# A chunked recurrence in twelve slots per pair of heads: the side work moved behind the state product, and row steps exchanged between VectorE and GpSimd

## The chip, the cores and the metric

The kernel runs on one core of a Trainium2 chip. The metric is the device time of one execution in microseconds (us), as the median of a few runs. The profile is one further execution, recorded by the hardware profiler. Engine names in its rows: PE is TensorE (matmuls), PEld its weight loads, DVE is VectorE, ACT is ScalarE, POOL is GpSimd, SP only issues DMAs.

## The reference, cut to what matters

The program is two transformer blocks. The change touches one stage of the second: the bidirectional recurrence (RWKV-7) over 768 tokens (512 of the sequence, 256 of a context) for 16 heads of width 64. Token by token, and for both directions, the reference computes:

```python
kk = heads(k * k_k);  kk = kk / maximum(norm(kk), 1e-12)
kt = heads(k)[None] * (1 + (a - 1) * heads(k_a))
sk = einsum('bhij,bhj->bhi', S, kk)                       # one step
S  = S * w - sk[..., None] * kka + v[..., None] * kt
y  = einsum('bhij,bhj->bhi', S, r)
```

where `kka` is `kk * a`. The outputs `y` of both directions are added, normalised per head, scaled and shifted (`ln_g`, `ln_b`), a bonus `(r * kt * r_k) summed * v` is added, and all is multiplied by a gate `g`.

## The kernel before

The 16 heads are worked two at a time: eight *pairs*, p = 0 to 7 (`RW_PAIRS`). Within a pair the 768 tokens are cut into twelve chunks of 64, in both directions at once. A chunk is one *slot*, i = 0 to 11 (`RW_STEPS`). A slot carries the state of the recurrence on, and that is a chain that no order can shorten:

1. PE multiplies the state with the chunk's keys (`scan_u`, matmuls L3651);
2. DVE adds the chunk's own part and gives `u` (`scan_u`, L2773);
3. PE forms the state product from `u` (`scan_states`, L3678) and, in slots 4 to 11, the outputs (L3662, L3666, L3685);
4. DVE adds it to the state (L2780) and multiplies by the decay (L2783), and the next slot can begin.

Beside this chain each engine works for the next pair, n = p + 1, and in part for the one after, m = p + 2. Everything is written out by hand: each engine's program is a fixed list, and semaphores tie the lists together. There is no scheduler. `beside_values(p, i)` is what stands between `scan_u` and the state product of slot i, and `beside_states(p, i)` what stands behind the state product. The PSUM banks are handed out by a plan in the same order (`plan_recurrence`).

The side work for a pair, in the order in which it depends on itself:

- DVE makes unit keys (`unit_keys`, four parts, L2675 to L2684) in slots 5 to 8 of the pair before the previous one.
- GpSimd (`factors`, L1421 to L1426) forms `kk * a` and `k * (1 + (a - 1) * k_a)` for both directions, 768 elements a partition, then three products for the bonus (`weigh_bonus`, L1433 to L1435).
- PE makes cumulated decays by matmul (`side` with "sum" and "sum_ex", L3527 and L3531), ACT takes their exponentials (L1804 to L1808), DVE scales keys, factors and r by them (`scale`, L2703), PE turns the results (`side`, L3539) and ACT copies them out (L1812).
- In slot 3 PE forms the 32-row blocks (`blocks_of`, L3560), DVE masks them (L2724, L2732) and transposes them (L2737).
- GpSimd inverts the blocks by row steps (`invert_blocks`, L1446 and L1447: 30 steps of a multiply and a subtract, 30 to 240 elements a partition, each waiting for the one before).
- In slot 10 DVE transposes the result twice (`turn_blocks`, L2744 and L2745), and `join`, `inverse` and `solved` on PE and ACT (L3573, L3584, L3596, L3602) make of it what the slots of the next pair read.
- DVE reads out the pair before (`read_out` in five parts, L2797 to L2818) and forms v times bonus (`weigh_values`, L2767, L2768).

Where an instruction waits on a result of its own engine the helper `link` puts a semaphore between the two. The buffer `products_kept` holds both the bonus products and the temporary of the row steps; the keys `kk` and the untransposed `blocks` share their memory.

Of the kernel before, what the change touches and what calls it, by code (L numbers as in the profile page):

```python
# [18 lines left out]
ALU = mybir.AluOpType  # L19
# [399 lines left out]
RW_SCALED = [("K", 0), ("R", 0), ("B", 0), ("T", 0), ("B", 1), ("K", 1), ("R", 1), ("T", 1)]  # L419
# [10 lines left out]
def plan_recurrence(plan, norm):  # L430
# [26 lines left out]
    def beside_values(p, i):  # L457
# [3 lines left out]
        if i == 0:  # L461
            if goes_on:
                side(n, "R", 0, 2)
            if p >= 0:
                plan.add("act", "rw_x", p, 1, width=4, bank=4)
        elif i == 1:
            if p >= 0:
                plan.add("act", "rw_inv", p, 1, width=4, bank=4)
            if goes_on:
                side(n, "T", 0, 2)  # L470
        elif i == 2:
            if p >= 0:
                solved(p, 1)
            if goes_on:
                side(n, "B", 1, 2)
        elif i == 3 and goes_on:
            plan.add("dve", "rw_lead", n, width=2, bank=4)
            plan.add("act", "rw_off", n, width=2, bank=6)
        elif i == 4 and p >= 0:
            plan.add("act", "rw_inv", p, 2, width=4, bank=4)  # L480
        elif i == 5 and p >= 0:
            solved(p, 2)
        elif i == 6 and goes_on:
            plan.add("act", "rw_gv", n, 0, width=2, bank=6)
# [8 lines left out]
    def beside_states(p, i):  # L493

        n = p + 1
        goes_on = n < RW_PAIRS
        if i == 0 and goes_on:
            side(n, "B", 0, 2)
            side(n, "sum", 1, 6)
        elif i == 1 and goes_on:  # L500
            side(n, "sum_ex", 1, 2)
        elif i == 2:
            if goes_on:
                side(n, "K", 1, 2)
            if p >= 0:
                plan.add("act", "rw_x", p, 2, width=4, bank=4)
        elif i == 3 and goes_on:
            plan.add("dve", "rw_tail", n, width=2, bank=4)
            side(n, "R", 1, 2)
        elif i == 4 and goes_on:  # L510
            side(n, "T", 1, 4)
        elif i == 5 and goes_on:
            plan.add("dve", "rw_g", n, 0, width=2, bank=4)
        elif i == 6 and goes_on:
            plan.add("dve", "rw_g", n, 1, width=2, bank=6)
        elif i == 7 and goes_on:
# [14 lines left out]
    for p in range(-1, RW_PAIRS):  # L531
        for i in range(RW_STEPS):
            if p >= 0:
                plan.add("dve", "rw_u", p, i, bank=0)
            beside_values(p, i)
            if p >= 0:
                scan_states(p, i)
            beside_states(p, i)
# [92 lines left out]
def build(nc, a, out, debug=None):  # L631
# [438 lines left out]
    def _(sp):  # L1070
# [14 lines left out]
        def load_beside(p):  # L1085
# [6 lines left out]
            if m < RW_PAIRS:  # L1092
# [4 lines left out]
                sp.wait_ge(sem("rw_factors"), factored(n, "T", 1))  # L1097
# [6 lines left out]
                sp.wait_ge(sem("rw_scaled"), rw_scaled(n, "T", 1))  # L1104
# [92 lines left out]
    def _(pool):  # L1197
# [211 lines left out]

        def factors(p, z):  # L1410
# [11 lines left out]
            pool.wait_ge(sem("rw_factors"), factored(p, "B", z))  # L1422
# [3 lines left out]
            G.tensor_tensor(az, az, RW_IN["k"], ALU.mult).then_inc(sem("rw_factors"), 1)  # L1426

        def weigh_bonus(p):
# [3 lines left out]
            pool.wait_ge(sem("rw_factors"), factored(p, "T", 1))  # L1432
# [4 lines left out]
        def invert_blocks(p):  # L1437

            pool.wait_ge(sem("rw_blocks_turned"), p + 1)
            link(G.memset(Y.rearrange("p c r -> p (c r)")[:, 0:SUB * SUB:SUB + 1], -1.0))  # L1440
            pool.wait_ge(sem("rw_bonus_ready"), p + 1)
            for j in range(1, SUB - 1):
                shape = [P, j, SUB - 1 - j]
                rest = Y[:, 0:j, j + 1:SUB]
                kept = products_kept.rearrange("p t d -> p (t d)")[:, 0:j * (SUB - 1 - j)].rearrange("p (c r) -> p c r", c=j)
                link(G.tensor_tensor(kept, Y[:, j:j + 1, j + 1:SUB].to_broadcast(shape), Y[:, 0:j, j:j + 1].to_broadcast(shape), ALU.mult))  # L1446
                ins = G.tensor_tensor(rest, rest, kept, ALU.subtract)  # L1447
                if j < SUB - 2:
# [2412 lines left out]
```

## Time and profile before

| | us |
|---|---|
| runs (three) | 4464.9, 4474.24, 4474.59 |
| median | 4474.24 |
| profiled execution | 4468.43 |
| its span on the core | 4467.1 |
| busy in the span: PE / DVE / ACT / POOL | 3969.7 / 1493.4 / 1030.2 / 1244.3 |
| the recurrence: from the first state (pair 0) to the first state of pair 7 | 639.2, seven pairs |

Outside the recurrence PE is busy for nine tenths of nearly every slice of the span. Inside it PE falls to six or seven tenths, and the granted clock of PE with it. The rest of the 4467 us is not touched by the change. A pair's start can be found in the trace by the memset of the state (L2788), a slot's start by the add that gives `u` (L2773).

### The profile page before, as it was taken

Reading aid. Unit: us, or ns where it says so; the run is one execution under the profiler, and the core shown is the slowest. Engines: PE = TensorE matmul, PEld = TensorE weight load, DVE = VectorE, ACT = ScalarE, POOL = GpSimd, SP = SyncE. Lnnn points to the kernel's source line nnn. Section 1 sums busy time; section 2 is a strip of 40 time slices with the busy share of each in tenths; the row PEclk is TensorE's granted clock in tenths of the full one; section 3 lists DMA queues with packets and bytes.
Section 4 is the critical chain, followed back from the end, with each engine's and each line's share of the span. In section 5 each row is a group of like instructions: output and inputs, shape, how many; then the busy total and the mean of one; then the engine's idle time right before and its main releaser. Section 6 shows DMA issues by size and latency. Waiting matters only on the chain.

```text
span 4467.1 us, 80505 instructions
## 1 busy us (share of the span) xinstructions
PE 3969.7 (89%) x34715; PEld 2496.1 (56%) x34715; DVE 1493.4 (33%) x2904; ACT 1030.2 (23%) x2164; POOL 1244.3 (28%) x1239
## 2 busy tenths in 40 slices
PE   8999999998999899997999998997566677769999
PEld 7977887877887444663333333444445555433443
DVE  4333332333243220553100115024455555342223
ACT  1032111002201221551212222113333333131111
POOL 4324323423344102110011110115666566010000
PEclk9999999999999999998999999998777777789999
DMA  4244212222222212552899996325011110169999
GB/s 152 88 169 148 83 60 75 76 99 82 84 94 81 65 57 59 161 156 102 309 344 344 348 346 252 101 96 173 28 31 38 46 35 10 46 250 409 408 406 368
DMA packets 277214, 701.52 MB, mean 157 GB/s; under 512 B 27488, under 2 KB 78080, under 8 KB 276608
## 3 DMA queue, kind: packets, MB, share of 16 engines
q1 hardware_dynamic: 250608, 637.58, 38.9%
q0 software_dynamic: 26256, 58.79, 4.9%
q8 instruction: 279, 4.57, 0.4%
q14 instruction: 71, 0.58, 0.0%
HBM read 654.61 MB, written 38.93 MB: 155 GB/s over the span
## 4 chain that ended last, share of the span: by engine, by line
PE 34%; POOL 6%; issue 5%; DVE 4%; DMA 4%; ACT 2%; SPq 0%; POOLq 0%; DVEq 0%; ACTq 0%
PE banks L3384 9%; PE banks L2951 6%; PE banks L3410 4%; DMA ring<-in_moe_w 3%; PE banks L3394 3%; POOL arena L1447 2%; POOL arena L1446 2%; PE banks L3357 2%; PE banks L3704 1%; PE banks L3418 1%; PE banks L3502 1%; ACT arena L1727 1%; PE banks L3493 1%; PE banks L3527 1%; PE banks L3475 1%
## 5 line engine op out<-in xcount | busy, mean ns | idle before, releaser
L2951 PE MATMUL banks<-ring,arena 128*128 128x512 f32 x1248 | 541.8, 594 | 0.4 <-DVE arena L2435 0.4
L2992 PE MATMUL banks<-arena 128*128 128x256 f32 x2256 | 507.7, 381 | 6.0 <-DVE arena L1990 6.0
L3384 PE MATMUL banks<-ring,arena 128*64 128x512 f32 x2048 | 471.4, 600 | 13.0 <-DMA ring<-in_moe_w 6.9
L2992 PEld LDWEIGHTS banks<-arena 128*128 128x128 f32 x2256 | 436.6, 200 | 61.3 <-issue 5.5
L2951 PEld LDWEIGHTS banks<-ring,arena 128*128 128x128 f32 x1248 | 236.0, 191 | 288.6 <-issue 285.8
L2992 PE MATMUL banks<-ring,arena 128*128 128x256 f32 x1584 | 356.3, 383 | 1.6 <-DVE arena L2299 1.6
L2992 PEld LDWEIGHTS banks<-ring,arena 128*128 128x128 f32 x1584 | 314.9, 216 | 35.6 <-DVE arena L2299 2.4
L3384 PEld LDWEIGHTS banks<-ring,arena 128*64 128x64 f32 x2048 | 140.2, 137 | 325.8 <-issue 318.0
L1249 POOL TENSOR_TENSOR arena<-ring 128x1024 f32<-128x1024 f32 x47 | 117.1, 2491 | 642.9 <-PE banks L2992 627.2
L2992 PE MATMUL banks<-arena,ring 128*128 128x256 f32 x1280 | 283.0, 379 | 1.2 <-ACT arena L1579 0.7
L3410 PE MATMUL banks<-ring,arena 128*64 128x512 f32 x1024 | 262.6, 665 | 6.9 <-ACT arena L1748 6.6
L2992 PEld LDWEIGHTS banks<-arena,ring 128*128 128x128 f32 x1280 | 243.2, 190 | 35.6 <-issue 1.4
L2589 DVE TENSOR_TENSOR arena<-banks,arena 64x512 f32<-64x512 f32 x64 | 44.4, 694 | 566.0 <-ACT arena L1741 566.0
L1741 ACT ACTIVATE arena<-banks 64x512 f32<-64x512 f32 x64 | 37.7, 589 | 591.6 <-PE banks L3384 591.6
L3410 PEld LDWEIGHTS banks<-ring,arena 128*64 128x64 f32 x1024 | 81.9, 152 | 153.3 <-issue 143.1
L2562 DVE TENSOR_TENSOR arena<-arena,banks 128x512 f32<-128x512 f32 x112 | 70.7, 683 | 257.3 <-PE banks L3357 257.3
L1447 POOL TENSOR_TENSOR arena<-arena 128x30 f32<-128x30 f32 (+14 forms) x240 | 144.5, 602 | 18.8
L1258 POOL TENSOR_TENSOR arena<-ring,arena 128x1024 f32<-128x1024 f32 x47 | 119.5, 2543 | 98.2 <-PE banks L2992 96.3
L1990 DVE TENSOR_TENSOR arena<-arena 128x1024 f32<-128x1024 f32 x55 | 116.8, 2124 | 85.8 <-PE banks L2992 80.7
L1446 POOL TENSOR_TENSOR arena<-arena 128x30 f32<-128x30 f32 (+14 forms) x240 | 133.8, 558 | 18.8
L3539 PE MATMUL banks<-ident,arena 64*64 64x64 f32 x2816 | 80.1, 279 | 66.3 <-DVE arena L2703 53.4
L1727 ACT ACTIVATE arena<-banks,mod,mod_a 128x64 f32<-128x64 f32 (+1 forms) x384 | 117.5, 422 | 65.8 <-PE banks L3311 35.5
(460 smaller groups left out, 5750.5 us busy)
## 6 DMA issues: line engine op xcount, KB each, us to landing
ring<-in_moe_w SPq DMA_DIRECT2D x768, 512.0 KB, 8.9
ring<-in_w_in SPq DMA_DIRECT2D x21, 2048.0 KB, 7.7
ring<-in_ada_w SPq DMA_DIRECT2D x12, 2048.0 KB, 8.0
ring<-in_ada_w SPq DMA_DIRECT2D x24, 1024.0 KB, 5.6
ring<-in_w_up SPq DMA_DIRECT2D x8, 2048.0 KB, 8.6
ring<-in_w_down SPq DMA_DIRECT2D x8, 2048.0 KB, 7.8
ring<-in_na_w_qkv SPq DMA_DIRECT2D x6, 2048.0 KB, 8.0
ring<-in_w_in SPq DMA_DIRECT2D x8, 1024.0 KB, 6.4
```

The costliest lines, as they stand in the source:

```text
L1249: nc.gpsimd.tensor_tensor(s1, a21, a22, ALU.add).then_inc(sem("weights_added"), 1)
L1258: nc.gpsimd.tensor_tensor(s4, a12, s2, ALU.subtract).then_inc(sem("weights_added"), 1)
L1446: link(G.tensor_tensor(kept, Y[:, j:j + 1, j + 1:SUB].to_broadcast(shape), Y[:, 0:j, j:j + 1].to_broadcast(shape), ALU.mult))
L1447: ins = G.tensor_tensor(rest, rest, kept, ALU.subtract)
L1727: ins = A(x_chosen[:, b, 4 * half + k, lo:hi], ps[:, k, lo:hi], ACT.Identity, bias=shift, scale=scale)
L1990: V.tensor_tensor(to, x, y, ALU.subtract).then_inc(sem("tokens_added"), 1)
L2951: ins = mm(ps[:, 0:ncol], lhs(k), rhs(k), start=(k == 0 and first), stop=(k == nk - 1))
L2992: ins = mm(ps[:, HW * j:HW * (j + 1)], lhs[:, k, j, :] if len(lhs.shape) == 4 else lhs[:, k, P * j:P * (j + 1)], rhs[:, k, :], start=(star ...
L3357: ins = mm(open_("moe_add", l, e, kind, t, n), selT[rows, b, t * P:(t + 1) * P], y_l[rows, b, :], start=True, stop=True)
L3384: ins = mm(ps, x_chosen[:, b, k, 0:CAP_L], w[x][:, n * W:(n + 1) * W], start=(k == 0), stop=(k == KD - 1))
L3394: ins = mm(ps[r:r + CAP_C, :], x_chosen[:, b, k, CAP_L:SLOTS], w[:, n * W:(n + 1) * W], start=(k == 0), stop=(k == KD - 1))
L3410: ins = mm(ps, hidT[:, k, 0:CAP_L], w[:, n * W:(n + 1) * W], start=(k == 0), stop=(k == KD - 1))
```

## The change

Three things change.

First the order. `beside_values` and `beside_states` become one `beside(p, i)` on every engine, behind the state product:

```diff
             for i in range(RW_STEPS):
                 if p >= 0:
                     scan_u(p, i)
-                beside_values(p, i)
-                if p >= 0:
                     scan_values(p, i)
                     scan_states(p, i)
-                beside_states(p, i)
+                beside(p, i)
```

Some products move to another slot with it: "sum_ex" of direction 1 from slot 1 to 0, "B" of direction 0 from 0 to 1, "T" of direction 0 from 1 to 2, the tail blocks stand right behind the lead blocks in slot 3, `join(p, 2)` goes from slot 2 to 1, "sum" and "sum_ex" of pair m to slots 8 and 9, its "K" to slot 10.

Second the row steps go from GpSimd to DVE, cut over slots 4 to 9:

```diff
-        def invert_blocks(p):                                  # GpSimd
...
+        def invert_blocks(p, lo, hi):                          # VectorE
+            if lo == 1:
+                dve.wait_ge(sem("rw_blocks_turned"), p + 1)
+            for j in range(lo, hi):
...
+                link(V.tensor_tensor(kept, Y[:, j:j + 1, j + 1:SUB].to_broadcast(shape), Y[:, 0:j, j:j + 1].to_broadcast(shape), ALU.mult))
+                link(V.tensor_tensor(rest, rest, kept, ALU.subtract))
```

Third, streaming work goes from DVE to GpSimd: the weighing of the keys, their scaling to unit length, the scaling of "T" of direction 1, the last three products of the read-out and the two of v times bonus. In `factors` two operations with a constant become operations with a tensor:

```diff
-            link(G.tensor_scalar(az, az, -1.0, None, ALU.add))
             link(G.tensor_tensor(az, az, across(k_a, NT), ALU.mult))
-            link(G.tensor_scalar(az, az, 1.0, None, ALU.add))
-            G.tensor_tensor(az, az, RW_IN["k"], ALU.mult)
+            link(G.tensor_tensor(az, az, across(k_a, NT), ALU.subtract))
+            link(G.tensor_tensor(az, az, RW_IN["k"], ALU.mult))
+            G.tensor_tensor(az, az, RW_IN["k"], ALU.add)
...
-        for p in range(RW_PAIRS):
-            factors(p, 1)
-            weigh_bonus(p)
-            invert_blocks(p)
-            if p + 1 < RW_PAIRS:
-                factors(p + 1, 0)
+        for p in range(-1, RW_PAIRS):
+            n, m = p + 1, p + 2
+            if n < RW_PAIRS:
+                factors(n, 1)
+                scale_values(n)
+                weigh_bonus(n)
+            if m < RW_PAIRS:
+                weigh_keys(m)
+                scale_keys(m)
+            if p >= 1:
+                read_out(p - 1)
+            if p >= 0:
+                weigh_values(p)
+            if m < RW_PAIRS:
+                factors(m, 0)
```

`weigh_keys(m)` waits for `rw_blocks_turned` of pair n (slot 3), `scale_keys(m)` for the new semaphore `rw_key_scales` (DVE, slot 8), `read_out` for `rw_y_scaled` (DVE, slot 8), `factors(m, 0)` for PE's "sum_ex" of pair m (slot 9), `factors(n, 1)` for the last output of pair n - 2. The waits of ACT, PE and SP on the scaled "T" of direction 1 now name the semaphore of the factors.

On PE, slot 3 of one pair before, with the end of slot 2; L3651 is the product that opens a slot, L3560 the blocks, L3678 the state product, L3539 a turned operand:

```order
L3678 MATMUL banks<-ring,arena 64x64 x4
L3678 MATMUL banks<-arena 64x64 x4
L3539 MATMUL banks<-ident,arena 64x64 x24
L3573 MATMUL banks<-arena 32x32 x16
L3651 MATMUL banks<-arena,ring 64x128 x2
L3560 MATMUL banks<-arena 32x32 x96
L3678 MATMUL banks<-ring,arena 64x64 x4
L3678 MATMUL banks<-arena 64x64 x4
L3560 MATMUL banks<-arena 32x32 x48
L3539 MATMUL banks<-ident,arena 64x64 x16
L3651 MATMUL banks<-arena,ring 64x128 x2
```

The same place in the changed kernel (L3661 opens the slot, L3570 the blocks, L3688 the state product, L3549 a turned operand):

```order
L3606 MATMUL banks<-arena,ring 64x64 x16
L3612 MATMUL banks<-ring,arena 64x64 x16
L3549 MATMUL banks<-ident,arena 64x64 x48
L3661 MATMUL banks<-arena,ring 64x128 x2
L3688 MATMUL banks<-ring,arena 64x64 x4
L3688 MATMUL banks<-arena 64x64 x4
L3570 MATMUL banks<-arena 32x32 x144
L3661 MATMUL banks<-arena,ring 64x128 x2
```

The 96 block products that stood between `u` and the state product now stand behind it, together with the other 48.

On DVE, slot 8 of a pair before; L2773 to L2783 are the chain, L2682 to L2684 the keys, L2811 to L2813 the read-out:

```order
L2773 TENSOR_TENSOR arena<-banks,ring 128x128
L2780 TENSOR_TENSOR arena<-banks,arena 128x256
L2783 TENSOR_TENSOR arena<-arena 128x256
L2682 TENSOR_SCALAR rw_s<-rw_s 128x12
L2683 RECIPROCAL rw_s<-rw_s 128x12
L2684 TENSOR_TENSOR arena<-arena,rw_s 128x768
L2811 RECIPROCAL rw_s<-rw_s 128x8
L2812 TENSOR_TENSOR ring<-ring,rw_s 128x512
L2813 TENSOR_TENSOR ring<-ring,arena 128x512
```

Slot 8 in the changed kernel, up to its third row step (L2797 to L2807 are the chain, L2767 and L2768 the row steps, of which this slot has seven):

```order
L2797 TENSOR_TENSOR arena<-banks,ring 128x128
L2804 TENSOR_TENSOR arena<-banks,arena 128x256
L2807 TENSOR_TENSOR arena<-arena 128x256
L2705 TENSOR_SCALAR rw_s<-rw_s 128x12
L2706 RECIPROCAL rw_s<-rw_s 128x12
L2835 RECIPROCAL rw_s<-rw_s 128x8
L2836 TENSOR_TENSOR ring<-ring,rw_s 128x512
L2767 TENSOR_TENSOR arena<-arena 128x234
L2768 TENSOR_TENSOR arena<-arena 128x18x13
L2767 TENSOR_TENSOR arena<-arena 128x228
L2768 TENSOR_TENSOR arena<-arena 128x19x12
```

Two wide operations have left the slot and fourteen small ones have come.

On GpSimd, what stands in the changed kernel from the bonus products on (L1410 and L1416 the keys, L1464 to L1466 the read-out, L1455 and L1456 v times bonus, L1427 to L1432 the factors); before, the 60 row steps followed the bonus products here, and then the factors:

```order
L1448 TENSOR_TENSOR arena<-arena 128x512
L1410 TENSOR_TENSOR arena<-ring,arena 128x768
L1416 TENSOR_TENSOR arena<-arena,rw_s 128x768
L1464 TENSOR_TENSOR ring<-ring,arena 128x512
L1465 TENSOR_TENSOR ring<-ring,arena 128x512
L1466 TENSOR_TENSOR ring<-ring 128x512
L1455 TENSOR_TENSOR arena<-ring,arena 128x512
L1456 TENSOR_TENSOR arena<-arena 128x512
L1427 TENSOR_TENSOR ring<-arena,ring 128x768
L1429 TENSOR_TENSOR ring<-ring,arena 128x768
L1430 TENSOR_TENSOR ring<-ring,arena 128x768
```

Everything GpSimd does for a pair is now wide operations with two tensors as inputs, 21 of them.

## Rows read from the trace of the kernel before

**Rows 1.** Windows: PE, PEld, DVE, ACT, POOL busy us (count), clock, DMA share, GB/s.

```profile
3167.88:3807.06 639.18, 433.74 (x12360) 343.92 (x12360) 356.79 (x537) 212.84 (x445) 409.38 (x516) 0.73 0.12 35
3361.82:3384.91 23.09, 15.29 (x464) 11.54 (x464) 13.34 (x19) 8.98 (x18) 7.25 (x5) 0.84 0.27 84
3384.91:3396.84 11.93, 7.93 (x372) 6.75 (x372) 4.74 (x8) 1.72 (x5) 0.00 (x0) 0.50 0.05 18
3396.84:3421.19 24.35, 18.51 (x588) 15.35 (x578) 16.84 (x28) 9.24 (x20) 21.50 (x37) 0.83 0.06 19
3421.19:3427.30 6.11, 4.12 (x72) 3.56 (x72) 5.22 (x11) 1.73 (x4) 5.56 (x8) 0.72 0.01 3
3427.30:3431.41 4.11, 3.72 (x33) 1.95 (x33) 3.13 (x5) 2.46 (x5) 3.72 (x6) 0.69 0.00 0
3431.41:3441.86 10.45, 5.38 (x60) 3.86 (x60) 6.40 (x8) 2.69 (x6) 9.34 (x16) 0.83 0.12 39
3441.86:3450.96 9.10, 6.17 (x205) 5.19 (x208) 3.72 (x5) 4.27 (x10) 8.84 (x5) 0.78 0.17 46
```

**Rows 2.** Waits from 3167.88 to 3807.06: us in total, times, longest.

```profile
POOL arena L1440 <- DVE arena L2737: 185.0, 7, 29.4
DVE arena L2780 <- PE banks L3678: 134.4, 70, 4.2
DVE arena L2773 <- PE banks L3651: 75.3, 30, 6.5
```

**Rows 3.** Timeline, DVE, opening of slot 8: start, duration, what, idle before.

```profile
3421.19 0.28 DVE L2773 TENSOR_TENSOR arena<-banks,ring 128x128 f32<-128x128 f32 x1
3422.12 0.43 DVE L2780 TENSOR_TENSOR arena<-banks,arena 128x256 f32<-128x256 f32 x1 [0.65 <-PE banks L3678]
3422.58 0.75 DVE L2783 TENSOR_TENSOR arena<-arena 128x256 f32<-128x256 f32 x1
```

**Rows 4.** One line's instructions on DVE: duration ns min/median/max, first and last start.

```profile
L2711 DVE TENSOR_TENSOR arena<-arena x16: 172/488/1799, 3100.3 to 3746.3; 128x24 f32<-128x24 f32 x16
L2780 DVE TENSOR_TENSOR arena<-banks,arena x88: 414/425/426, 3179.0 to 3872.1; 128x256 f32<-128x256 f32 x88
L2703 DVE TENSOR_TENSOR arena<-arena x24: 958/961/2487, 3086.8 to 3745.4; 128x768 f32<-128x768 f32 x24
```

**Rows 5.** Groups on POOL, same stretch: count, busy us, mean ns, idle before.

```profile
L1424 POOL TENSOR_TENSOR ring<-ring,arena 128x768 f32<-128x768 f32 x14 | 25.4, 1817 | 1.2
L1446 POOL TENSOR_TENSOR arena<-arena 128x240 f32<-128x240 f32 x14 | 8.8, 631 | 1.1
```

**Rows 6.** Timeline, DVE and POOL in slot 0.

```profile
3362.53 1.81 POOL L1426 TENSOR_TENSOR ring<-ring 128x768 f32<-128x768 f32 x1
3363.61 1.00 DVE L2783 TENSOR_TENSOR arena<-arena 128x256 f32<-128x256 f32 x1
3364.48 1.26 POOL L1433 TENSOR_TENSOR arena<-ring 128x512 f32<-128x512 f32 x1
3364.65 3.67 DVE L2703 TENSOR_TENSOR arena<-ring,arena 128x768 f32<-128x768 f32 x2
3365.82 1.69 POOL L1434 TENSOR_TENSOR arena<-arena,ring 128x512 f32<-128x512 f32 x1
3367.59 1.87 POOL L1435 TENSOR_TENSOR arena<-arena 128x512 f32<-128x512 f32 x1
```

**Rows 7.** Timeline, DVE and POOL in slot 0 of the next pair.

```profile
3453.96 2.18 POOL L1425 TENSOR_SCALAR ring<-ring 128x768 f32<-128x768 f32 x1
3454.19 2.33 DVE L2703 TENSOR_TENSOR arena<-ring,arena 128x768 f32<-128x768 f32 x2
3456.22 1.96 POOL L1426 TENSOR_TENSOR ring<-ring 128x768 f32<-128x768 f32 x1
3456.44 1.79 DVE L2711 TENSOR_TENSOR arena<-arena 128x24 f32<-128x24 f32 x1
```

**Rows 8.** Timeline, DVE ahead of pair 0.

```profile
3163.84 1.97 DVE L2744 STREAM_TRANSPOSE arena<-arena 128x1024 f32<-128x1024 f32 x1 [20.23 <-POOL arena L1447]
```

More of the change, by code:

```diff
@@ L465, in beside_values @@
                 plan.add("act", "rw_x", p, 1, width=4, bank=4)
+            if goes_on:
+                side(n, "sum", 1, 4)
+                side(n, "sum_ex", 1, 6)
         elif i == 1:
+            if goes_on:
+                side(n, "B", 0, 2)
             if p >= 0:
                 plan.add("act", "rw_inv", p, 1, width=4, bank=4)
+                plan.add("act", "rw_x", p, 2, width=4, bank=4)
             if goes_on:
-                side(n, "T", 0, 2)
+                side(n, "B", 1, 2)
         elif i == 2:
@@ new lines, in beside @@
+            plan.add("dve", "rw_g", n, 2, width=2, bank=4)
+        elif i == 8:
+            if goes_on:
+                plan.add("act", "rw_gv", n, 2, width=2, bank=6)
+            if n + 1 < RW_PAIRS:
+                side(n + 1, "sum", 0, 4)
+        elif i == 9 and n + 1 < RW_PAIRS:
+            side(n + 1, "sum_ex", 0, 6)
+        elif i == 10:
+            if n + 1 < RW_PAIRS:
+                side(n + 1, "K", 0, 6)
+            if p >= 1 and goes_on:
+                plan.add("act", "rw_ot", p - 1, bank=4)
@@ L1408, in across, with weigh_keys, scale_keys @@
             return row.unsqueeze(1).to_broadcast([P, nt, P])
+        def weigh_keys(p):
+            loaded(pool, "k", p)
+            loaded(pool, "rows", p)
+            if p >= 1:
+                pool.wait_ge(sem("rw_blocks_turned"), p)
+                pool.wait_ge(sem("rw_scaled"), rw_scaled(p - 1, "K", 1))
+            G.tensor_tensor(kk, RW_IN["k"], across(rw_rows[:, 0, :], NT), ALU.mult).then_inc(sem("rw_keys_weighed"), 1)
+        def scale_keys(p):
+            pool.wait_ge(sem("rw_key_scales"), p + 1)
+            keys = kk.rearrange("p t (h d) -> p (t h) d", d=HD)
+            G.tensor_tensor(keys, keys, rw_s[:, 0:12].unsqueeze(2).to_broadcast([P, 12, HD]), ALU.mult).then_inc(sem("rw_keys_ready"), 1)
+            pool.wait_ge(sem("rw_keys_ready"), p + 1)
         def factors(p, z):
@@ L1460, in _ @@
+        read_out(RW_PAIRS - 1)
         taken(pool, "rw_ot", RW_PAIRS - 1)
@@ L1877, in beside_values @@
                     joined(p, 1)
+                if goes_on:
+                    side(n, "sum", 1)
+                    side(n, "sum_ex", 1)
             elif i == 1:
+                if goes_on:
+                    side(n, "B", 0)
                 if p >= 0:
                     inverse(p, 1)
+                    joined(p, 2)
                 if goes_on:
-                    side(n, "T", 0)
+                    side(n, "B", 1)
             elif i == 2:
@@ L2900, in _ @@
                     scan_u(p, i)
-                beside_values(p, i)
-                if p >= 0:
                     scan_state(p, i)
-                beside_states(p, i)
-        for part in range(1, 6):
+                beside(p, i)
+        for part in range(1, 5):
             read_out(RW_PAIRS - 1, part)
@@ L3716, in beside_values @@
                     join(p, 1)
+                if goes_on:
+                    side(n, "sum", 1)
+                    side(n, "sum_ex", 1)
             elif i == 1:
+                if goes_on:
+                    side(n, "B", 0)
                 if p >= 0:
                     inverse(p, 1)
+                    join(p, 2)
                 if goes_on:
-                    side(n, "T", 0)
+                    side(n, "B", 1)
             elif i == 2:
@@ L3725, in beside_values @@
                 if goes_on:
-                    side(n, "B", 1)
+                    side(n, "K", 1)
+                    side(n, "T", 0)
             elif i == 3 and goes_on:
@@ L3741, in beside_values @@
                 group_values(n, 1)
-            elif i == 10 and n + 1 < RW_PAIRS:
-                side(n + 1, "sum_ex", 0)
+                rb_products(n, 2)
+                g_products(n, 2)
+            elif i == 8:
+                if goes_on:
+                    group_values(n, 2)
+                if n + 1 < RW_PAIRS:
+                    side(n + 1, "sum", 0)
+            elif i == 9 and n + 1 < RW_PAIRS:
+                side(n + 1, "sum_ex", 0)
+            elif i == 10:
+                if n + 1 < RW_PAIRS:
+                    side(n + 1, "K", 0)
+                if p >= 1 and goes_on:
+                    read_out(p - 1)
             elif i == 11 and goes_on:
```

365 lines of the change are left out of this document (149 added, 216 removed).

## The prediction

> **What bounds the kernel now.** I read the page first: PE is nine tenths busy nearly everywhere but in the recurrence, so only there can a new order be worth anything. Then the windows. From the first state of pair 0 to that of pair 7 seven pairs take 639.2 us, 91.3 us each; in them PE is busy 434, POOL 409, DVE 357 [rows 1]. No engine is full, so the pair is bound by a chain that changes engine. The seven further windows cut one pair at its slots (3361.82 to 3450.96, 89.1 us): slots 0 to 3 take 35.0 us (23.1 and 11.9), slots 4 to 9 34.6 us (24.35, 6.11 and 4.11), slots 10 and 11 19.55 us [rows 1].
>
> The waits say which chain. DVE waits for the state product 134.4 us in 70 slots, 1.92 us a slot, and for the product that gives `u` another 75.3 us [rows 2]. Where nothing stands between `u` and the state product the first wait is 0.65 us [rows 3]. So 1.27 us a slot is PE's side work in front of the state product: 12.7 us for the ten such waits of a pair. POOL is no bound: it waits 26.4 us a pair for the blocks [rows 2], and takes 58.5 [rows 1]. But a faster pair would run into it: 60 row steps of up to 0.63 us [rows 5] must fit between slot 3 and slot 10.
>
> **The change part by part.**
>
> *The order.* It takes away at most the 12.7 us above. Not all comes back: the products still have to be made, now beside DVE's side work. In slots 0 to 3, 10 and 11 PE and ACT set the end; by the windows they take 54.55 us. In slot 3 PE is busy 7.9 of 11.9 us, and behind its last block DVE still has to mask and transpose; slot 0 now also gets "sum_ex". I credit half of 12.7, 6.3 us, there. What it gives in slots 4 to 9 is in the next sum, which starts from nothing but DVE's work.
>
> *Row steps on DVE.* Prices: 24 elements take 0.17 us, 256 take 0.425, 768 take 0.96 [rows 4]; that is 0.15 us and 1.05 ns an element, and 0.04 us to the next linked operation (L2780 ends at 3422.55, L2783 stands at 3422.58 [rows 3]). Thirty steps of j x (31 - j) elements, twice, are 9920 elements: 10.4 us, and 60 x 0.19 = 11.4 us, together 21.8 us of DVE a pair. Off DVE go two operations of 768 for the keys, one of 768 for "T", three of 512 for the read-out, two of 512 for v times bonus: 3 x 0.96 + 5 x 0.69 = 6.3 us at undisturbed prices. DVE's total of 51 us a pair [rows 1] becomes some 66.
>
> Slots 4 to 9 hold all of it. A slot there costs DVE the chain, 0.28 + 0.65 + 0.43 + 0.04 + 0.42 = 1.82 us [rows 3], and then its side work, since `u` of the next slot stands behind that. Six chains are 11; row steps 21.8; masks, key sums and the three read-out parts that stay, 10.7 (three masks of 512, two double ones, two operations of 768, six of 512 or small). That is 43.5 us where the windows show 34.6: 8.9 us worse. With the 6.3 us above, a pair without any disturbance between DVE and POOL is 2.6 us longer.
>
> *Streaming on POOL.* This decides. In slot 0 DVE and POOL take turns. L2783, 0.42 us alone, takes 1.00, until POOL's L1426 ends at 3364.34; two L2703 of 0.96 take 3.67, while POOL's 1.09 and 1.26 us operations become 1.69 and 1.87 [rows 6]. Twenty-four elements take 1.79 us and end with POOL's operation [rows 7]. So an operation with two SBUF inputs on one engine waits out such an operation on the other, and between two of one the other gets its turn. Each POOL operation that falls among row steps therefore delays DVE by its own length, 1.82 [rows 5] or 1.26 us [rows 6], plus 0.08 to the next, less the 0.45 us of the DVE operation that fits in: 1.45 us at 768 wide, 0.9 at 512.
>
> Where do they fall? `weigh_keys` waits for the transposed blocks: slot 4, one operation, 1.45. `scale_keys`, three of the read-out and two of v times bonus are released by DVE in slot 8, in front of its 14 row operations: 1.45 + 5 x 0.9 = 5.95, and slot 8 has enough operations to meet all six. `factors(m, 0)` starts when PE has done "sum_ex" in slot 9, when three or four of the 12 row operations there are left, and goes on under the transposes of slot 10: 4.0 (between 1 and 7). Slots 0 to 2 see such operations before and after. Sum 11.4 us a pair. All of it is on the path: PE's side work in slots 8 and 9 is 4 us or less, and `u` is queued on DVE behind the row steps.
>
> The low end of this term is 0, if the operations miss each other or POOL does not get a turn inside a linked row; the high end is all that POOL does between slot 8 and slot 10, 1.82 + 5 x 1.26 + 1.54 + 4 x 1.82, 17 us. I take 11.4, which is rows 6 applied as it stands.
>
> The Trainium skill (SBUF — State Buffer, SBUF: two separate sides) has DVE and GpSimd share a port pair as an exclusive lock for a whole instruction, against any GpSimd operation that reads SBUF. By that the constants' operations held DVE just as well, and replacing them changes nothing. The trace disagrees in part: beside the one-input L1425 two L2703 took 2.33 us, not 1.92 and a wait of 2 us [rows 7]. By the page some of my slot 9 term was paid before too, and the sum would be up to 2 us a pair lower, 4541; by the row four operations a pair are new blockers, and 4555 stands.
>
> *Head and tail.* Ahead of pair 0 DVE waits 20.2 us for POOL's row steps [rows 8]. They shrink from about 38 (3126 to 3163.8) to 21.8 plus what stands between them on DVE, some 10; but the unit keys of pair 0 now wait for POOL, about 4 us. I take -4, between -18 and +5. The last read-out waits for three POOL operations of 1.26 instead of 0.69: +2.
>
> *Sum.* Pairs 1 to 5: 2.6 + 11.4 = 14, times five, 70. In pair 0 there is no read-out, 14 - 2.7 = 11.3. In pair 6 there is no pair m: no keys, five POOL operations at 0.9 against 3.5 us less on DVE, about +4. Together 85, with head and tail 83. On the profiled execution (4468.4) that is 4551; the median of the runs lies 6 us above it, so I say 4555 against 4474.
>
> **The rivals.**
>
> *A, faster: the chain was the bound and DVE has room.* Mechanism: in every slot PE's side work now runs beside DVE's, and POOL's wide operations fall on DVE's PSUM reads and waits, not among the row steps. Price: -12.7 in full against +8.9, -3.8 a pair, 27 us in seven, and 15 us of the 20.2 us at the head: 4432. For it: 134 us of waits at the state product. Against: the row steps are two-input operations nearly back to back. It decides if slot 8 takes 9 us or less.
>
> *B, the exchange is even: no turns taken, but DVE is full in slots 4 to 9.* 7 x 2.6 - 2: +16, 4490. For it: POOL's 34 us a pair leave it idle most of the time.
>
> *C, worse: POOL gets late.* `read_out` and `factors(m, 0)` are delayed by DVE as DVE is by them; if `factors(n, 1)` then begins only in slot 0, the scaling of "B" and PE's turned operands wait too. Price: the whole 17 us instead of 11.4, and some 4 us in slots 0 to 2: 10 more a pair, 4620.
>
> *D, nothing:* A and B cancel within 0.3% (13 us, what a measurement of this kernel can tell), around 4474.
>
> **How the numbers follow.** Forecast 0.53, its own range 4510 to 4595. A 0.21, B 0.11, C 0.07, D 0.08. Faster by over 0.3%: A, 0.21. Within: D, 0.08. Slower: the rest, 0.71. The range to hold eight in ten goes from 4440, inside A, to 4600.
>
> **What the changed profile would show.** Right: the wait of DVE for the state product near 0.65 us in nearly every slot; slot 8 of a middle pair 13 to 17 us with POOL and DVE durations alternating, row operations there over 1 us each where those of slots 6 and 7 are near 0.4; slots 5 to 7 between 7 and 8.5 us; slot 3 under 11; a pair of 103 to 107 us. POOL idle before `scale_keys`, not before anything else for long. Wrong: row operations in slot 8 near 0.4 us beside a busy POOL (then B), slots 0 to 3 under 28 us together (then A), or POOL releasing "B" late (then C). It would also be wrong if a linked row operation on DVE cost not 0.19 us and 1.05 ns an element: 0.1 us more each is 6 us a pair.

## The result and the profile after

| | before | after |
|---|---|---|
| median of four runs | 4469.57 us (4464.12 to 4474.59) | 4560.63 us (4552.72 to 4566.39) |
| profiled execution | 4468.43 us | 4566.39 us |
| span | 4467.1 us | 4565.0 us |
| first state of pair 0 | 3167.9 us | 3176.0 us |
| seven pairs | 639.2 us | 737.9 us |
| from the first state of pair 7 to the end | 660.0 us | 651.1 us |

The changed kernel is slower: ratio 1.0211, with a 95% interval of 1.019 to 1.0232. The forecast was 4555 us. The changed profiled execution is 98 us longer: 98.7 us more in the seven pairs, 8.2 more ahead of them, and 8.9 less behind them.

In what follows the line numbers of a kernel are its own: in the changed kernel `u` is L2797, the state's add L2804 and its decay L2807, the row steps are L2767 and L2768, `scale` is L2725, the state's memset L2812. A *turn* is what an operation of one vector engine loses while it waits for an operation of the other to end.

Page of the changed kernel, its first line: busy us, share of the span and instructions of each engine.

```profile
PE 3996.9 (88%) x34715; PEld 2533.2 (55%) x34715; DVE 1630.5 (36%) x3328; ACT 1031.4 (23%) x2164; POOL 1040.6 (23%) x815
```

Windows of the changed kernel, which answer to [rows 1]: the seven pairs, then pair 2 cut into slots 0 to 3, slots 4 to 9, slot 10 and slot 11.

```profile
3176.04:3913.92 737.88, 463.64 (x12372) 380.99 (x12372) 463.36 (x911) 213.15 (x445) 204.26 (x132) 0.67 0.10 31
3397.55:3431.72 34.17, 23.50 (x784) 18.67 (x784) 16.48 (x26) 9.51 (x18) 7.56 (x6) 0.70 0.23 74
3431.72:3481.69 49.97, 31.15 (x748) 25.44 (x748) 42.15 (x97) 15.70 (x33) 9.94 (x8) 0.76 0.04 10
3481.69:3494.79 13.10, 4.36 (x95) 3.73 (x92) 8.86 (x7) 2.41 (x6) 8.55 (x5) 0.56 0.01 1
3494.79:3503.34 8.55, 6.05 (x152) 4.85 (x148) 1.26 (x3) 3.45 (x9) 6.67 (x4) 0.50 0.16 48
```

DVE is busy 463 us in the seven pairs and was 357; POOL is down from 409 to 204. PE is busy 30 us more with the same products, at a granted clock of 0.67 against 0.73. The pair shown takes 105.8 us (pairs 1 to 5 take 105.7 to 109.1). Against the pair of [rows 1], slots 0 to 3 take 0.8 us less, slots 4 to 9 15.4 us more (DVE is busy for 42.15 of the 49.97 us), slots 10 and 11 2.1 us more. The pair of [rows 1] is the fastest of pairs 1 to 5 of its kernel. By the means of pairs 1 to 5 slots 4 to 9 again take 15.4 us more, and the other six slots 0.1 us less.

Waits in the changed kernel from 3176 to 3914, which answer to [rows 2]: us in total, times, longest.

```profile
POOL arena L1416 <- DVE rw_s L2706: 178.0, 6, 29.9
DVE arena L2797 <- PE banks L3661: 147.0, 41, 9.1
POOL arena L1410 <- DVE arena L2757: 136.5, 6, 24.7
DVE arena L2804 <- PE banks L3688: 61.7, 77, 2.2
POOL ring L1427 <- PE banks L3538: 59.6, 6, 11.2
POOL arena L1427 <- PE banks L3695: 34.2, 6, 5.9
```

The order did what it was to do: DVE waits 0.80 us a slot for the state product (61.7 us in 77 waits) where it waited 1.92. It waits for `u` instead, 147 us where it was 75. POOL is idle in front of both operations on the keys (L1410, L1416) and in front of the factors (L1427).

Timeline of the changed kernel, DVE and POOL in slot 8, which answers to [rows 3] and [rows 5], with one operation of slot 7 above it and `u` of slot 9 at its end.

```profile
3455.70 0.41 DVE L2767 TENSOR_TENSOR arena<-arena 128x238 f32<-128x238 f32 x1
...
3463.46 1.47 POOL L1416 TENSOR_TENSOR arena<-arena,rw_s 128x768 f32<-128x768 f32 x1 [29.72 <-DVE rw_s L2706]
3463.48 2.00 DVE L2836 TENSOR_TENSOR ring<-ring,rw_s 128x512 f32<-128x512 f32 x1
3465.61 1.31 POOL L1464 TENSOR_TENSOR ring<-ring,arena 128x512 f32<-128x512 f32 x1 [0.68 <-POOL arena L1416]
3465.82 1.35 DVE L2768 TENSOR_TENSOR arena<-arena 128x234 f32<-128x234 f32 x1
...
3468.38 1.30 POOL L1466 TENSOR_TENSOR ring<-ring 128x512 f32<-128x512 f32 x1
3468.59 1.34 DVE L2768 TENSOR_TENSOR arena<-arena 128x228 f32<-128x228 f32 x1
...
3470.91 1.29 POOL L1456 TENSOR_TENSOR arena<-arena 128x512 f32<-128x512 f32 x1
3471.11 1.33 DVE L2768 TENSOR_TENSOR arena<-arena 128x220 f32<-128x220 f32 x1
3472.48 0.38 DVE L2767 TENSOR_TENSOR arena<-arena 128x210 f32<-128x210 f32 x1
...
3475.61 0.29 DVE L2797 TENSOR_TENSOR arena<-banks,ring 128x128 f32<-128x128 f32 x1
```

Each row operation beside POOL lasts until POOL's operation is over, and ends 0.2 us after POOL's next one has started (3467.17 and 3467.00 the first time): 1.35 us for 234 elements, where 238 take 0.41 alone. Five are held for POOL's five operations of 512, and L2836 for `scale_keys`. When POOL is done, at 3472.2, the row operations are back at 0.38. The slot takes 14.56 us, from `u` at 3461.05 to `u` at 3475.61.

Slot 10, DVE and POOL, also of the changed kernel:

```profile
3481.39 1.54 POOL L1427 TENSOR_TENSOR ring<-arena,ring 128x768 f32<-128x768 f32 x1 [9.19 <-PE banks L3538]
3483.06 2.03 DVE L2807 TENSOR_TENSOR arena<-arena 128x256 f32<-128x256 f32 x1
...
3489.21 2.16 DVE L2725 TENSOR_TENSOR arena<-arena 128x768 f32<-128x768 f32 x1
3494.79 0.29 DVE L2797 TENSOR_TENSOR arena<-banks,ring 128x128 f32<-128x128 f32 x1 [3.42 <-PE banks L3661]
```

The factors begin at 3481.39, 0.2 us behind the last row operation of slot 9. So their turns fall on the decay, 2.03 us for 0.42, and on the scaling of "K", 2.16 for 0.96. Then DVE waits 3.42 us for `u`: PE has to transpose "K" in front of it, and "K" came only behind both of DVE's transposes.

PE transposing "K" in this slot (timeline of PE from 3481 to 3496), and a transposed operand at the end of slot 2 of the same pair (from 3415 to 3432):

```profile
3491.52 1.56 PE L3549 MATMUL banks<-ident,arena 64*64 64x64 f32 x48 [8.74 <-DVE arena L2725]
3417.76 0.92 PE L3549 MATMUL banks<-ident,arena 64*64 64x64 f32 x46 [0.25 <-issue]
```

PE had stood idle for 8.74 us when "K" came. From 3491.4 to the end of slot 11 the granted clock is 0.50, the lower of TensorE's two levels (1.2 GHz), and the 48 products take 1.56 us. Where the granted clock is 1.00 (3417.2 to 3418.6) 46 such products take 0.92. So part of the 3.42 us, and of slot 11's 8.55 us, is the slower clock behind the long wait.

### The profile page after: what moved, and what is told of

Same layout as the page of the kernel before. It is cut to its first block, busy times and chain, and to the rows that moved or that the text cites. A ratio compares the mean times of both kernels' runs of the same rounds, so it can differ in the third digit from the quotient of the medians.

```text
span 4565.0 us, 80518 instructions
## 1 busy us (share of the span) xinstructions
PE 3996.9 (88%) x34715; PEld 2533.2 (55%) x34715; DVE 1630.5 (36%) x3328; ACT 1031.4 (23%) x2164; POOL 1040.6 (23%) x815
## 4 chain that ended last, share of the span: by engine, by line
PE 35%; DVE 10%; DMA 5%; issue 3%; ACT 2%; POOL 1%; SPq 0%; DVEq 0%; POOLq 0%; ACTq 0%
PE banks L3391 9%; PE banks L2958 6%; DMA ring<-in_moe_w 4%; PE banks L3417 3%; PE banks L3401 3%; DVE arena L2768 2%; DVE arena L2767 2%; PE banks L3364 2%; PE banks L3549 1%; PE banks L3425 1%; PE banks L3534 1%; PE banks L3688 1%; PE banks L3714 1%; ACT arena L1755 1%; PE banks L3500 1%
## 5 line engine op out<-in xcount | busy, mean ns | idle before, releaser
L3549 PE MATMUL banks<-ident,arena 64*64 64x64 f32 x2816 | 80.4, 287 | 105.2 <-DVE arena L2725 89.0
L3688 PE MATMUL banks<-ring,arena 64*64 64x64 f32 x704 | 39.0, 290 | 131.7 <-DVE arena L2797 130.2
L3549 PEld LDWEIGHTS banks<-ident,arena 64*64 64x64 f32 x2816 | 73.5, 196 | 108.7 <-issue 93.4
```

The source lines that it names most:

```text
L3549: ins = mm(ps[to, c, t * CH:(t + 1) * CH], x[rows, t, to], ident[rows, rows], start=True, stop=True)
```

## The experiments

Ratios are against the kernel before, run beside on the same chip; its medians there were 4461.5 to 4465.8 us, so differences between medians of two experiments carry up to 8 us of that against 4469.57. Slot times are of one middle pair, where not called means. Since single executions reach the recurrence at times that differ by up to 8 us, its head is measured from GpSimd's memset of 128 x 256 just ahead of it (L1468 in the changed kernel): 80.1 us to the first state before, 88.4 us after. Means of pairs 1 to 5, in us:

| | slots 0 to 3 | 4 to 9 | 10 | 11 | all but 4 to 9 | pair |
|---|---|---|---|---|---|---|
| before | 35.8 | 35.3 | 10.8 | 10.0 | 56.7 | 91.9 |
| changed | 35.0 | 50.7 | 13.0 | 8.6 | 56.5 | 107.2 |
| `order_only` | 33.7 | 37.6 | 13.4 | 7.3 | 54.5 | 92.1 |
| `exchange_only` | 36.3 | 53.9 | 8.4 | 9.2 | 53.9 | 107.8 |
| `no_streak` | 34.7 | 46.6 | 12.9 | 8.6 | 56.2 | 102.8 |
| `no_rows` | 34.6 | 34.4 | 12.1 | 7.8 | 54.5 | 88.9 |
| `order_k_first` | 34.3 | 37.6 | 8.4 | 8.1 | 50.7 | 88.3 |
| `after_k_first` | 35.2 | 51.1 | 9.9 | 8.0 | 53.1 | 104.1 |
| `after_constants` | 35.3 | 50.7 | 10.8 | 7.7 | 53.8 | 104.5 |
| `read_out_back` | 35.2 | 49.7 | 12.2 | 7.7 | 55.1 | 104.8 |
| `three_together` | 34.8 | 49.6 | 7.9 | 7.1 | 49.8 | 99.4 |

**Order alone** (`order_only`). The order and tables of the change, with the row steps on GpSimd, the streaming work on VectorE and the constants in the factors as before:

```diff
 scan_u(p, i)
-beside_values(p, i)
 scan_state(p, i)
-beside_states(p, i)
+beside(p, i)
 # row steps, keys, read-out, v times bonus: as before
```

> The order of the changed kernel (side work behind the state product, the products in their new slots) with the old split of the work: row steps on GpSimd, keys, read-out and v times bonus on VectorE. The theory in the prediction (VectorE full in slots 4 to 9, and VectorE and GpSimd taking turns there, is what costs): the loss must be gone, 4445 to 4475 us, that is within 0.5% of before; not much below, because the 38 us of row steps on GpSimd then set the time from slot 3 to slot 10. Rival A (the order is worth its full 12.7 us a pair): 4385 or less. Rival (the new order itself is what loses, since 'K' of pair m now stands in slot 10 behind the transposes): 4500 or more.

Measured: 4452.88 us, ratio 0.9983 (0.9971 to 0.9996). The order is worth next to nothing as written. Slots 0 to 3 take 34.1 us, slots 4 to 9 37.2 (2.6 more than before), slot 10 13.7. By the means it gives 2.2 us a pair outside slots 4 to 9 and takes 2.4 inside them; what is left of it is 5.0 us at the head (75.1 for 80.1) and 8.8 from the first state of pair 7 on (651.3 for 660.0).

**Exchange alone** (`exchange_only`). The old order; row steps on VectorE, streaming work on GpSimd, factors without constants:

```diff
-invert_blocks(p)                 # GpSimd
+invert_blocks(p, lo, hi)         # VectorE, in slots 4 to 9
-read_out parts, weigh_values     # VectorE
+read_out, weigh_values           # GpSimd
```

> The exchange alone (row steps on VectorE, streaming on GpSimd, factors without constants) in the old order, with the row steps cut over slots 4 to 9 as in the changed kernel. Theory: it carries the whole loss and more, since PE's side work in front of the state product is not hidden either: 4560 to 4640. Rival (the order loses, the exchange is even): 4470 to 4500.

Measured: 4577.91 us, ratio 1.0271 (1.0252 to 1.0289). The whole loss is the exchange's; the order gives 0.6% of it back (1.0271 to 1.0211), most of it at the head (98.9 us here, 88.4 in the changed kernel) and little in a pair (107.8 and 107.2).

**Without GpSimd's streak** (`no_streak`). It leaves out the last three products of the read-out and the two of v times bonus, but for 8 columns of one tile:

```diff
-link(G.tensor_tensor(d, d, across(ln_rows[:, p % 2, 0, :], LT), ALU.mult))
-link(G.tensor_tensor(d, d, vb, ALU.add))
-G.tensor_tensor(d, d, RW_G[p % 2], ALU.mult)
+G.tensor_tensor(d[:, 0, 0:8], d[:, 0, 0:8], RW_G[p % 2][:, 0, 0:8], ALU.mult)
```

> The changed kernel with GpSimd's five 512-wide operations of read-out and v times bonus cut down to two operations of 8 elements each; the read-out's last products and v times bonus are left out. VectorE's own work is the same. Theory (turns): the row operations of slot 8 fall from 1.3 to 0.4 us, slot 8 from 14.6 to 10 us, 4 to 5 us a pair, 25 to 35 us in all: 4525 to 4535. Rival (VectorE is slow there by its own work, GpSimd does not hold it): 4560, no change.

Measured: 4528.38 us, ratio 1.015 (1.0131 to 1.0169), 32 us under the changed kernel. Slot 8 falls from 14.6 to 10.0 us: 4.5 us for five operations, 0.9 each. The row operation that took 1.35 us above, here:

```profile
3455.89 0.45 DVE L2764 TENSOR_TENSOR arena<-arena 128x234 f32<-128x234 f32 x1
```

Over a whole pair the gain is 4.4 us.

**Without the row steps** (`no_rows`). It leaves out the 30 row steps; all else is the changed kernel's:

```diff
-for j in range(lo, hi):
+for j in range(0):
```

> The changed kernel without any of the 60 row operations a pair (the blocks are not inverted). Theory: they are 21.8 us of VectorE on the path and the hosts of the turns (5 us in slot 8), but without them PE's side work sets slots 4 to 9 at about 5 us each: 20 to 25 us less a pair, eight times with the head, 4370 to 4400. Rival (PE and ACT set the pair and VectorE had room): 4500 or more.

Measured: 4411.02 us, ratio 0.99 (0.9877 to 0.9924); 11 us above what was expected. The row steps and what they meet cost 150 us. But slots 4 to 9 fall only to 34.5 us, not below 30: with its row steps gone DVE waits up to 3.1 us for PE's products, so in this kernel PE sets the end of slots 4 to 6.

**"K" ahead of the transposes**, in the order-only kernel (`order_k_first`) and in the changed one (`after_k_first`):

```diff
 elif i == 10:
-    if goes_on: turn_blocks(n)
     if follows: scale(m, "K", 0)
+    if goes_on: turn_blocks(n)
```

> order_only with one exchange on VectorE in slot 10: the scaling of 'K' of pair m stands in front of the two transposes of the blocks, not behind them. Theory: in order_only the first u of slot 11 waits 3.4 us on PE, which turns 'K' only after VectorE's 4 us of transposes and a disturbed 2.5 us scaling; in front of the transposes that hides, and in their 2.1 us wait for GpSimd. Slot 10 from 13.7 to 9 or 10 us, seven pairs, some 25 to 30 us: 4420 to 4430, faster than before by about 1%. Rival (slot 10 is set by GpSimd's row steps and ACT, not by 'K'): 4450, no change against order_only.

> The changed kernel with the same exchange in slot 10. Theory: slot 10 from 13.1 to about 10 us (u waits 3.4 us less; the scaling still meets GpSimd), 6 pairs: 4538 to 4545. Rival (no part of the loss comes from slot 10's order): 4560.

Measured: 4420.72 us, ratio 0.9899 (0.9883 to 0.9916), the fastest version that computes everything; and 4542.63 us, ratio 1.0173 (1.0156 to 1.019). Windows of `order_k_first`, its seven pairs:

```profile
3157.05:3768.43 611.38, 428.43 (x12324) 355.70 (x12324) 353.45 (x536) 212.53 (x444) 417.61 (x516) 0.74 0.12 37
```

Its slot 10, timeline of DVE:

```profile
3408.41 0.99 DVE L2687 TENSOR_TENSOR arena<-arena 128x768 f32<-128x768 f32 x1
3410.65 2.00 DVE L2728 STREAM_TRANSPOSE arena<-arena 128x1024 f32<-128x1024 f32 x1 [1.24 <-POOL arena L1438]
...
3414.64 0.24 DVE L2757 TENSOR_TENSOR arena<-banks,ring 128x128 f32<-128x128 f32 x1
```

"K" (L2687) now runs in the time in which DVE waited for POOL's row steps, and `u` (L2757) follows the transposes with no wait, since PE transposed "K" under them. Slots 0 to 3, 10 and 11 together take 48.8 us against 54.55 before, by the means 50.7 against 56.7: 5.7 to 5.9 of the 6.3 us a pair that the prediction credited to the order. The order as it was made had given most of it away in slot 10.

**Constants back** (`after_constants`). The two operations with a tensor become again two with a constant:

```diff
-link(G.tensor_tensor(az, az, across(k_a, NT), ALU.subtract))
-link(G.tensor_tensor(az, az, RW_IN["k"], ALU.mult))
-G.tensor_tensor(az, az, RW_IN["k"], ALU.add)
+link(G.tensor_scalar(az, az, 1.0, None, ALU.add))
+G.tensor_tensor(az, az, RW_IN["k"], ALU.mult)
```

with a `tensor_scalar(az, az, -1.0, None, ALU.add)` ahead of them.

> The changed kernel with GpSimd's factors as before: two of the four operations have a constant in place of the second tensor (2.13 us each in place of 1.81). Theory, by the row in which two L2703 took 2.33 us beside a one-input operation: those do not hold VectorE, so L2807 in slot 10 falls from 2.03 to about 0.5 us and the scaling of 'K' from 2.2 to about 1.0: 2 to 3 us a pair less, 4540 to 4550. Rival, by the Trainium skill (SBUF — State Buffer, SBUF: two separate sides), which has the shared ports locked against any GpSimd operation that reads SBUF: no gain, 4560 to 4565, since each operation holds VectorE 0.3 us longer.

Measured: 4527.7 us, ratio 1.0134 (1.0117 to 1.0151), 33 us under the changed kernel where 10 to 20 were expected, though each such operation takes 2.13 us for 1.81. Of it 17.7 us are in the seven pairs and 10.8 at the head, which the expectation had not counted. Slot 10 falls from 13.1 to 10.9: the scaling of "K" takes 0.96 us, as expected, and the decay 1.06, where about 0.5 was expected. Slot 11 falls from 8.55 to 7.49 with no change in its work. Windows of slot 11 in `after_constants` and in `order_only`:

```profile
3473.58:3481.07 7.49, 4.92 (x152) 3.82 (x148) 1.26 (x3) 3.45 (x9) 5.73 (x4) 0.73 0.18 55
3430.16:3437.41 7.25, 4.29 (x152) 3.35 (x148) 1.25 (x3) 3.45 (x9) 5.93 (x4) 0.90 0.17 58
```

The 152 products are those of the changed kernel's slot 11, which ran at a granted clock of 0.50: 8.55, 7.49 and 7.25 us at 0.50, 0.73 and 0.90. So about 1 us a pair of this experiment's gain came by the clock, and not by DVE's turns. The head of the changed kernel, DVE and POOL:

```profile
3154.66 1.54 POOL L1427 TENSOR_TENSOR ring<-arena,ring 128x768 f32<-128x768 f32 x1 [6.05 <-PE banks L3538]
3154.78 1.57 DVE L2768 TENSOR_TENSOR arena<-arena 128x130 f32<-128x130 f32 x1
3156.28 1.81 POOL L1429 TENSOR_TENSOR ring<-ring,arena 128x768 f32<-128x768 f32 x1
3156.39 1.83 DVE L2767 TENSOR_TENSOR arena<-arena 128x108 f32<-128x108 f32 x1
...
3169.19 1.80 POOL L1431 TENSOR_TENSOR ring<-ring 128x768 f32<-128x768 f32 x1
3169.21 1.84 DVE L2768 TENSOR_TENSOR arena<-arena 128x30 f32<-128x30 f32 x1
```

and the same place with the constants back:

```profile
3149.04 1.54 POOL L1427 TENSOR_TENSOR ring<-arena,ring 128x768 f32<-128x768 f32 x1 [6.39 <-PE banks L3538]
3149.15 1.56 DVE L2767 TENSOR_TENSOR arena<-arena 128x108 f32<-128x108 f32 x1
3150.67 2.13 POOL L1429 TENSOR_SCALAR ring<-ring 128x768 f32<-128x768 f32 x1
3150.74 0.88 DVE L2768 TENSOR_TENSOR arena<-arena 128x108 f32<-128x108 f32 x1
3151.66 0.25 DVE L2767 TENSOR_TENSOR arena<-arena 128x84 f32<-128x84 f32 x1
...
3152.97 1.78 DVE L2768 TENSOR_TENSOR arena<-arena 128x30 f32<-128x30 f32 x1
```

Ahead of pair 0 no chain holds the row steps apart, so the last nine meet the factors of pair 1 one for one: thirty elements take 1.84 us. Beside the one-input L1429 six row operations ran: the first in 0.88 us for 0.27, the five behind it at 0.21 to 0.25. So in these rows a one-input operation on GpSimd delays VectorE once, by 0.6 us (and so on the decay of slot 10, 1.06 for 0.42), and a two-input one holds each operation of VectorE for nearly its whole length. The one-input operation waits too: in `order_only` L1416 took 2.72 us for 2.13 beside a scaling of 768. The Trainium skill (SBUF — State Buffer, SBUF: two separate sides) has the lock on the port pair that both engines share hold against any GpSimd operation that reads SBUF; by that the first of the six would have lasted until L1429 ended at 3152.8, and it ended at 3151.62. Here page and measurement differ, and the measurement decides.

**Read-out back on VectorE** (`read_out_back`), the five operations of 512:

```diff
+link(V.tensor_tensor(d, d, over(ln_rows[:, p % 2, 0, :], LT), ALU.mult))
+link(V.tensor_tensor(d, d, vb, ALU.add))
+V.tensor_tensor(d, d, RW_G[p % 2], ALU.mult)        # slot 8
+weigh_values(p)                                     # slot 9, VectorE
```

> The changed kernel with the five 512-wide operations of read-out and v times bonus back on VectorE (slots 8 and 9). Theory: five times 0.73 us more on VectorE, five turns of 0.9 us less, that is 1 us a pair less or nothing: 4545 to 4562. Rival (work moved off the full engine is a gain whatever its neighbour does): 25 us slower than the changed kernel, 4585.

Measured: 4545.81 us, ratio 1.018 (1.0163 to 1.0197), 15 us under the changed kernel. In its slot 8, timeline of DVE:

```profile
3455.97 0.69 DVE L2835 TENSOR_TENSOR ring<-ring 128x512 f32<-128x512 f32 x1
3456.58 0.40 DVE L2762 TENSOR_TENSOR arena<-arena 128x234 f32<-128x234 f32 x1
3457.01 0.40 DVE L2763 TENSOR_TENSOR arena<-arena 128x234 f32<-128x234 f32 x1
```

The three products cost DVE 0.73 us each with the step to the next; on GpSimd each had cost it 0.9. Here it is cheaper for VectorE to do a 512-wide operation than to be beside it. By the means a pair is 2.4 us shorter, 1.0 of it in slots 4 to 9, which is what the theory has at the most; the rest is in slots 10 and 11.

**The three together** (`three_together`): "K" first, constants back, read-out and v times bonus back on VectorE. Its edit is the three diffs above.

> The changed kernel with three parts undone at once: the scaling of K stands in front of the block transposes in slot 10, the two operations with a constant are back in GpSimd's factors, and the three last products of the read-out and the two of v times bonus are back on VectorE. The row steps stay on VectorE. If each of the three turns taken is a loss of its own, the gains measured one by one (18, 33 and 15 us) add up: 4560.6 - 66 = 4495. If they share a stretch (both the K order and the constants shorten slot 10, 3 and 2.2 us a pair, and slot 10 cannot fall below some 8 us), the sum falls short by about 2 us a pair: 4505 to 4515. My theory, that what is left is then VectorE's own row steps in slots 4 to 9 (some 47 to 49 us for 37 in the kernel with the order alone), puts it 75 to 90 us above that kernel with K first (4420.7): 4495 to 4510. If turns on the shared memory were the whole loss, it would come near 4440.

Measured: 4501.09 us, ratio 1.0093 (1.0063 to 1.0123), 60 us under the changed kernel, where the three gains added up to 66, and 80 above `order_k_first`. By the means slots 4 to 9 take 49.6 us against 37.6 there, slots 10 and 11 15.0 against 16.5, slots 0 to 3 34.8 against 34.3. So what is left of the loss lies in slots 4 to 9, 12 us a pair, and 5.6 us at the head. Turns are left in it: `scale_keys` still costs 1.3 us in slot 8, and in pairs 0, 2 and 4 the factors meet v times bonus in slot 9, which takes 8.9 us there and 7.45 in pairs 1, 3 and 5. What remains after these, some 10 of the 12 us, is VectorE's own row steps with the five operations of 512 on the same engine; that is by subtraction, no run took it apart.

## Why the prediction was right, point by point

*The number and the sum.* 4555 us was forecast and 4560.6 measured. The sum itself said +83 us on the profiled execution, 4551, and 4566.4 was measured, +98. The 6 us added for the distance to the median went the other way in the changed kernel, whose median lies 5.8 us under its profiled execution. The mechanism, turns of DVE with POOL beside a full DVE, is what the runs show. That the number came so close is in part luck, since two terms were wrong with opposite signs.

*State-product wait near 0.65 us:* 0.80. Right.

*Row steps on DVE, 0.15 us and 1.05 ns an element:* 238 elements took 0.41 us, 30 took 0.21 in slot 9, with 0.03 to the next. Right. Slots 4 to 9 without turns were put at 43.5 us. Take the turns of slots 4 and 8 below off the 49.97 and it is 44.0.

*Turns, 11.4 us a pair, in slots 4 to 9.* Slot 8: 1.3 (L2836, 2.00 for 0.69) and 4.5 (`no_streak`), 5.8 against 5.95; the slot took 14.56, within 13 to 17, and slots 5 to 7 took 7.3, 8.1 and 7.2, within 7 to 8.5. Slot 4: 1.45 was said and 0.15 measured, since POOL's L1410 (3431.92, 1.82 us) fell into DVE's wait for the state product and only the decay's end met it (0.57 us for 0.42). Slot 9: 4.0 was said for it; nothing fell there, since the factors came behind the last row step, and 2.8 us fell in slot 10, 1.6 on the decay and 1.2 on "K". In all 8.8 us for 11.4. The prediction also put PE's side work in slots 8 and 9 at 4 us or less. In slot 9 it took 4.2 us in this pair and 5.3 in pair 1, where the granted clock was 0.50 and DVE waited 1.88 us for `u` behind its row steps: pairs 0, 1 and 5 take 7.45 us in slot 9, pairs 2 to 4 6.1 to 6.3.

*The order's 6.3 us a pair in slots 0 to 3, 10 and 11.* This step failed. These slots took 55.8 us against 54.55, where 48.25 was said: a loss of 1.3, in which 2.8 of turns in slot 10 are contained. By the means they took 56.5 against 56.7. The order alone gave 55.1 in this pair and 54.5 by the means, a third of what was credited; with "K" moved it gave 48.8 and 50.7. The new place of "K" in slot 10 was known, but the prediction did not ask who waits for it there: PE's transposing of "K" stands ahead of the next `u`, and DVE's 4 us of transposes ahead of "K". Slot 3 was to be under 11 us and took 12.57. Timeline of PE in it:

```profile
3419.94 0.72 PE L3570 MATMUL banks<-arena 64*32 64x32 f32 x60
3422.87 1.79 PE L3570 MATMUL banks<-arena 64*32 64x32 f32 x127 [2.21 <-issue]
3426.90 1.66 PE L3570 MATMUL banks<-arena 64*32 64x32 f32 x101 [2.24 <-issue]
```

The block products run in one piece, with two gaps of 2.2 us in which PE waited for nothing that the profile shows. Such gaps were there before too, 1.31 and 1.72 us, one of them in the state product. What they are was not tried, so what they cost slot 3 stays open.

*Two errors that cancelled.* Slots 4 to 9 came out 4.9 us lower than said (49.97 for 43.5 + 11.4), the other slots 7.6 higher (55.8 for 48.25), together 105.8 us for 103.1 by the sum, and within the 103 to 107 named, which pairs 4 and 5 are not (109.1 and 108.5). The means say the same: slots 4 to 9 lost 15.4 us for 20.3, the others gained 0.1 for 6.3. Pairs 1 to 5 lost 77 us for 70.

*Pair 0* lost 17.6 us for 11.3, *pair 6* 4.4 for 4. In pair 0 slots 4 to 9 took 46.9 us for 28.4: the sum took off the turns of the read-out that is not there, but took the loss of slots 4 to 9 from a pair that had one.

*Head:* said -4, between -18 and +5; measured +8.3, outside that range. The length of the row steps was right, the turns were left out there: the nine row operations beside the factors took 16.0 us together, where the same lengths take 2.2 alone. With the factors' constants back only three are held, and the head is 77.6 us, 2.4 under before.

*Tail:* said +2, measured -8.9. Pair 7 has no next pair, and the prediction says nothing of its slots. But in slots 6 to 9 of it PE's output projection (L3704, twelve products of 128 x 512, some 5.5 us) had stood ahead of the state product. In the kernel before, timeline of DVE in pair 7:

```profile
3845.62 0.42 DVE L2780 TENSOR_TENSOR arena<-banks,arena 128x256 f32<-128x256 f32 x1 [6.02 <-PE banks L3678]
3853.40 0.42 DVE L2780 TENSOR_TENSOR arena<-banks,arena 128x256 f32<-128x256 f32 x1 [6.01 <-PE banks L3678]
```

In the changed kernel, same pair:

```profile
3958.78 0.42 DVE L2804 TENSOR_TENSOR arena<-banks,arena 128x256 f32<-128x256 f32 x1 [0.62 <-PE banks L3688]
3964.73 0.29 DVE L2797 TENSOR_TENSOR arena<-banks,ring 128x128 f32<-128x128 f32 x1 [4.09 <-PE banks L3661]
```

Waits of 6 us for the state product became waits of 4 to 5 us for `u`. From `u` of slot 0 to `u` of slot 11 pair 7 takes 52.4 us for 59.1. `order_only` has the same end (651.3 us from the first state of pair 7), so this gain is the order's.

*The rivals.* A (DVE has room) is refuted by slot 8 at 14.56 us, B (no turns) by rows of 1.34 us. C (POOL late) is refuted: POOL waits for PE before the factors both times, 59.6 and 34.2 us. D (nothing) is refuted by the interval. The order as a whole was no cause of the loss, as `order_only` and `exchange_only` show; the place of "K" in it costs 18 us of the changed kernel's time (`after_k_first`). One sign failed: POOL was to be idle for long before `scale_keys` alone, and it also waits 136.5 us for the transposed blocks before `weigh_keys` (L1410).

## What to carry to other kernels

Before work moves from one vector engine to the other, list which operations of the two will stand beside each other: here a two-input operation on GpSimd cost a chain of small ones on VectorE nearly its whole length each time they met, 0.9 us net for one of 512 that VectorE does itself in 0.69. Where a product is moved to another slot, ask who waits for it there and what is queued ahead of it: two exchanged lines in slot 10 were worth 32 us, more than the whole reordering without them. Compare means over several pairs: the one pair cut at its slots before was 2.8 us shorter than the mean. Stretches without the chain, the head and the last pair, need a sum of their own.

## What the runs showed of the hardware

- On GpSimd an operation of 768 with one input and a constant took 2.13 us, one with two tensors 1.81; with the slower one in four places a pair the kernel was 33 us faster, most of it since VectorE runs beside it, some 1 us a pair by a higher granted clock in slot 11.
- The two engines' two-input operations alternated one for one: nine row operations of 30 to 130 elements at 1.56 to 1.85 us each, beside operations of 1.54 to 1.81.
- The same 152 products of slot 11 took 8.55, 7.49 and 7.25 us at granted clocks of 0.50, 0.73 and 0.90. In the slowest case PE had been idle 8.74 us in slot 10.
- Runs of 60 and 127 products of 64 x 32 on PE were each followed by a gap of 2.2 us that has no releaser in the trace. In slot 3 of the next pair gaps of 1.9, 2.3 and 1.2 us stand behind 36, 127 and 125 products.
